# Clearing the dispatch rows from the row tile between the two first attentions

## The reference

```
mod = silu(c) @ ada_w + ada_b                 # six vectors of 1024: shift1, scale1, gate1, shift2, scale2, gate2
h = rmsnorm(x, norm1_g) * (1 + scale1) + shift1
qa, ka, va, fa, qb, kb, vb, ga, gb = split(h @ w_in)
o_fox = forgetting_attention(qa, ka, va, log_sigmoid(fa + b_forget))     # 8 heads of 64
o_sb  = stick_breaking_attention(qb, kb, vb)                             # 8 heads of 64
merged = sigmoid(ga) * (o_fox @ w_branch_fox) + sigmoid(gb) * (o_sb @ w_branch_sb)
x = x + gate1 * (merged @ w_out)
h2 = rmsnorm(x, norm2_g) * (1 + scale2) + shift2
y = hierarchical_moe(h2, ...)   # 16 experts, top 1 of 4 groups, top 2 of its 4 experts
x = x + gate2 * y
```

## Time and profile before

| what | value |
|---|---|
| time, median of 3 runs | 2736.78 us (2731.76 to 2738.37) |
| the profiled execution, its own time | 2731.88 us |
| its span, first to last instruction | 2730.3 us |
| PE busy | 2325.5 us, 85% |
| DVE, ACT, POOL busy | 1027.8, 831.5, 224.7 us |
| mean granted clock of PE | 0.918 |

### The profile page before, as it was taken

The page is one execution under the profiler, slowest core; times in us unless marked ns, Lnnn a source line. Parts: engine busy times, 40 slices in busy tenths (PEclk is TensorE's granted clock), DMA queues, the critical chain, the costliest instruction groups (busy, mean ns, idle before and its releaser), DMA issues.

```text
span 2730.3 us, 25692 instructions
## 1 busy us (share of the span) xinstructions
PE 2325.5 (85%) x9810; PEld 1662.0 (61%) x9810; DVE 1027.8 (38%) x1436; ACT 831.5 (30%) x1311; POOL 224.7 (8%) x255
## 2 busy tenths in 40 slices
PE   7898989829999956988859989959999976899996
PEld 4667666614444425855648778848865545777785
DVE  5635623431101014333542334442345554323444
ACT  3344511211111113213432223432245443222332
POOL 0420010010000011001010000030212100100000
PEclk9999899969999987979979999979999988899998
DMA  9213093227898971201012222222100002222221
GB/s 355 77 37 118 22 355 102 77 86 269 301 323 312 313 264 48 95 19 55 31 54 93 91 78 93 94 78 92 49 2 1 1 1 69 78 80 90 93 93 46
DMA packets 156312, 309.57 MB, mean 113 GB/s; under 512 B 17966, under 2 KB 19763, under 8 KB 156213
## 3 DMA queue, kind: packets, MB, share of 16 engines
q1 hardware_dynamic: 131308, 259.50, 27.9%
q0 software_dynamic: 11520, 41.95, 3.9%
q10 hardware_dynamic: 13388, 6.80, 1.0%
HBM read 277.02 MB, written 30.99 MB: 113 GB/s over the span
## 4 chain that ended last, share of the span: by engine, by line
PE 77%; DVE 10%; ACT 4%; issue 3%; DMA 2%; POOL 1%; ACTq 1%; POOLq 0%; DVEq 0%; SPq 0%; PEldq 0%
PE PB L1498 44%; PE PB L1855 8%; PE PB L1874 4%; PE PB L2137 3%; PE PB L1483 2%; PE PB L2113 1%; DVE WL L2230 1%; PE PB L1938 1%; PE PB L1915 1%; PE PB L1715 1%; PE PB L2114 1%; DVE CI L2853 1%; DVE NAT L2748 1%; DVE X L2750 1%; PE PB L2076 1%
## 5 line engine op out<-in xcount | busy, mean ns | idle before, releaser
L2230 DVE TENSOR_TENSOR WL<-RING,WH 128x1024 fp32r<-128x1024 f32 x232 | 288.4, 1243 | 736.7 <-ACT WH L826 460.3
L826 ACT CAST WH<-RING 128x1024 fp32r<-128x1024 f32 x232 | 243.6, 1050 | 932.2 <-PE PB L1498 864.1
L1498 PE MATMUL PB<-HTH,WH 128*128 128x512 f32 x1056 | 422.4, 400 | 60.7 <-DVE WL L2230 26.0
L1498 PE MATMUL PB<-HTL,WH 128*128 128x512 f32 x1056 | 418.5, 396 | 0.0
L1498 PE MATMUL PB<-HTH,WL 128*128 128x512 f32 x1056 | 418.0, 396 | 0.0
L1498 PE MATMUL PB<-WH,HTH 128*128 128x512 f32 (+1 forms) x832 | 323.9, 389 | 49.8 <-DVE HTL L2233 42.2
L1498 PE MATMUL PB<-WH,HTL 128*128 128x512 f32 (+1 forms) x832 | 322.0, 387 | 0.0
L1498 PE MATMUL PB<-WL,HTH 128*128 128x512 f32 (+1 forms) x832 | 321.6, 387 | 0.0
L1498 PEld LDWEIGHTS PB<-HTH,WH 128*128 128x128 f32 x1056 | 203.3, 192 | 108.0 <-issue 36.6
L1855 PE MATMUL PB<-RING,HT 128*128 128x512 f32 x512 | 226.1, 600 | 9.3 <-DVE HT L2622 7.6
L1498 PEld LDWEIGHTS PB<-HTH,WL 128*128 128x128 f32 x1056 | 202.8, 192 | 43.5
(11 more groups left out here) (453 smaller groups left out, 2846.7 us busy)
## 6 DMA issues: line engine op xcount, KB each, us to landing
RING<-in_mlp_w SPq DMA_DIRECT2D x64, 1024.0 KB, 5.3
RING<-in_expert_w_gate SPq DMA_DIRECT2D x32, 1024.0 KB, 5.6
RING<-in_expert_w_up SPq DMA_DIRECT2D x32, 1024.0 KB, 5.6
RING<-in_expert_w_down SPq DMA_DIRECT2D x32, 1024.0 KB, 6.7
BIG<-in_ada_w SPq DMA_DIRECT2D x10, 2048.0 KB, 11.8
RING<-in_w_in SPq DMA_DIRECT2D x20, 1024.0 KB, 5.6
dispatch_rows<-BIG POOLq DMA_DIRECT2D x24, 512.0 KB, 22.3
RING<-in_a_w_in SPq DMA_DIRECT2D x10, 1024.0 KB, 5.1
```

Of the source, the lines that this page charges most:

```text
L826: ins = nc.scalar.copy(WH[:, q % 2], halves_of(n, q))
L1498: yield pe.matmul(dst, lhs, rhs, start=(start and n == 0), stop=(stop_ and n == 2))
L2230: ins = V.tensor_tensor(WL[:, q % 2], halves_of(n, q), WH[:, q % 2].bitcast(F32), ALU.subtract)
```

## The change

The zero tile is now `ROW` in place of the last 1024 columns of `BIG`. POOL no longer waits for the end of the sb attention before it clears the zero tile and issues the 31 copies; it waits for the eight small transfers out of `ROW` (`fs_in`). Clearing `NAT[:, 0, :]` stays behind the sb attention and now stands behind the 31 copies on POOL. ACT waits for all 31 copies before it loads `gate1` into `ROW`.

```diff
@@ -347,7 +347,7 @@
-    ZERO = BIG[:, 15360:16384]
+    ZERO = ROW[:, :]
@@ -984,6 +984,9 @@
             act.wait_ge(mod_io, 32)
+            act.wait_ge(zero_out, 16 * (ROWS // P + 1 + SPARE - 2))
+            for m in range(2):
+                act.wait_ge(y_out[m], 16)
             gain_row(row_on_all(mod_dram[0, 2 * D:3 * D]))
@@ -1305,10 +1308,9 @@
             pool.wait_ge(fs_done, len(FOX_BLOCKS))
             nc.gpsimd.memset(SQ2[DH:P, :, :].bitcast(F32), 0.0).then_inc(f_pads, 1)
             pool.wait_ge(f_pads, 9)
-            pool.wait_ge(acc_done, GR["qkv"] + 8)
-            pool.wait_ge(sb_prod, len(SB_UNITS))
+            for par in range(2):
+                pool.wait_ge(fs_in[par], 16 * (NH1 // 2))
             nc.gpsimd.memset(ZERO, 0.0).then_inc(zeroed, 1)
-            nc.gpsimd.memset(NAT[:, 0, :], 0.0).then_inc(zeroed, 1)
             pool.wait_ge(zeroed, 2)
             for r in range(ROWS // P + 1):
                 pool.dma_start(disp[r * P:(r + 1) * P, :], ZERO).then_inc(zero_out, 16)
@@ -1317,6 +1319,9 @@
                 s = y_out[r % 2] if r < EXPERTS + 2 else zero_out
                 pool.dma_start(back[r * P:(r + 1) * P, :], ZERO).then_inc(s, 16)
+            pool.wait_ge(acc_done, GR["qkv"] + 8)
+            pool.wait_ge(sb_prod, len(SB_UNITS))
+            nc.gpsimd.memset(NAT[:, 0, :], 0.0).then_inc(zeroed, 1)
```

## The result

The changed kernel takes 2743.68 us (median of 13 runs, 2738.85 to 2747.30), the kernel before 2735.68 us (median of 13 timed with it, 2731.76 to 2743.83). The ratio is 1.0026, with a 95% interval of 1.0017 to 1.0034: slower by 7.1 us (4.6 to 9.3), and within the 0.3% that I took as the measure of "no change". The profiled execution took 2747.21 us, its span is 2745.6 us. It was one of the slowest of the changed kernel; what follows goes by stretches of the span, not by spans.

The account below looks back on a forecast made before the run. The prediction took PE to bound the kernel (busy 85% of the span). It summed -3.9 us at the gates and +11.2 at piece 9 to +7.3, on the median 2736.78 giving 2744 us, range 2733 to 2751.

Parts of the forecast that it names:

- Piece 9 beside the copies: Second projection: reads get 150 GB/s beside the copies, so piece 9 of `ada_w` lands at 252.5 instead of 236.9 us.
- Which other loads are covered: Around 204 to 260 us: piece 8 and chunks 9 and 10 may come late, but nothing waits for them.
- What is late then: From DVE's sums of piece 9 on: PE waits at part 20, and everything from part 22 stands 11.2 us later.
- The gates' gain: At the gates: one clearing less and piece 10 without copies beside it let PE restart earlier, -3.9 us.
- the low clock behind the gap: At the gates: PE's first 48 matmuls after the 3.7 us gap still lose 3.0 us to the low clock.
- a sign that it fails: At the gates: the prediction fails if PE's clock after the gap stays at 2.4 GHz.
- The sum: Whole kernel: -3.9 at the gates and +11.2 at piece 9 give +7.3 us.
- The copies' start: After the row sums leave `ROW`: first copy issued at about 199.5 us, bytes moving from about 204.5.
- What was to cost nothing: ACT's waits before the gain row and the late `NAT` clearing on POOL: both covered by the sb attention.
- Fairer turns: Rival at piece 9: equal bytes per queue, landing at 246.6, net +1.5 us, 2738; chance 0.17.
- Starvation: Rival at piece 9: it lands only once the copies are through, at 257, net +11.9 us, 2749; chance 0.17.
- No disturbance at all: Rival: copies disturb nothing at the new place, only the gates' gain stands, 2730 to 2733 us; chance 0.08.

Follow-up runs that it names:

- run 8: The changed kernel with piece 9 of `ada_w` read in 4 KB rows instead of 2 KB; piece 9 landed in 22.7 us; time not compared.
- run 4: The changed kernel with SP issuing piece 9 of `ada_w` ahead of chunk 11 of `w_in`; ratio 0.9985 against the kernel before, 2732.64 us.
- run 3: The changed kernel with POOL also waiting for piece 9 of `ada_w` to land before issuing the copies; ratio 0.9978 against the kernel before, 2731.03 us.
- run 7: The changed kernel with the first 12 copies left early and the other 19 behind piece 9's landing; ratio 0.9976 against the kernel before, 2730.09 us.
- run 5: The kernel before, zero tile still in `BIG`, with POOL waiting for piece 10 of `ada_w` to land before the copies; ratio 0.9990, 2732.99 us.

## Why the prediction was right

The sign and the mechanism were right, and so was the number (2744 against 2743.68); that it came so close is luck in part, as the sum below shows. Its steps, one by one:

- **Piece 9 beside the copies.** Predicted: lands 25.7 us after its issue. Measured: 26.4, 27.2 and 27.6. The step from the windows of 2 us to 150 GB/s held: beside the copies the reads had 0.30 MB in 2 us again.
- **Which other loads are covered.** Right: DVE went straight from its last step of the fox attention to piece 8 (215.27, 1.85 us later than before, of which 1.66 is the scatter ahead), and ACT waited for no chunk.
- **What is late then.** Predicted +11.2 us, with a gap of about 8.7 at part 20 and a small one before part 22. Measured: 9.26, 0.41 and 0.67, and +11.9 us; in the other two profiles of the change, 12.5 and 12.9 by the same landmark. PE's low clock behind the gap was hidden, as argued.
- **The gates' gain: right in kind, mis-sized.** Predicted -3.9; measured -6.4 in the first pair of profiles, and some -8 in the other two of the change. Two terms of it were off. The landing of an undisturbed piece 10 was taken from piece 8, 9.2 us; it was 7.7 to 8.0 in each run without copies beside it. Piece 8 was the wrong neighbour: it took 8.6 to 9.4 in all the profiles. And the low clock behind the gap was left at its full 3.0 us. PE took 12.8 us for the 48 matmuls in one profile of the change and 11.2 in the other two, in place of 13.9, so the clock cost 1.9 or 0.3 us. Windows over these 48 matmuls in the first and the second profile of the change (the last three figures are clock, DMA share and GB/s):

```profile
361.23:374.00 12.77, 12.77 (x49) 10.48 (x50) 5.37 (x6) 2.09 (x2) 0.00 (x0) 0.87 0.24 83
...
361.57:372.74 11.17, 11.17 (x49) 9.28 (x50) 5.37 (x6) 2.10 (x2) 0.00 (x0) 1.00 0.29 95
```

  In the second the clock stayed at 1.00 (2.4 GHz), which the prediction had named as a sign that it fails. It concerns this one term.
- **The sum.** +7.3 was predicted; the stretch gives +4.7 in the first pair of profiles (+3.9 on the means of three). Between them stand the two errors at the gates, 2.5 us together, less 0.7 at piece 9, and 0.8 us that the sb attention itself was shorter behind its new start (58.56 against 59.36 us from the fourth unit to the gates' first matmul), which I had not in the sum. The timed +7.1 is near the forecast only because it holds another 1 to 5 us, outside the stretch, that the prediction did not have. That part of the agreement is luck.
- **The copies' start.** The first copy was issued at 204.81, not 199.5: POOL stood for 4.62 us behind the clearing, where it had stood for 1.16 before. But the bytes then came 2.8 us after the issue, not 5, so they started at 207.6 in place of 204.5, and 1.66 us of these 3.1 are the scatter ahead. The copies ended at 261.2, not 256; piece 9 ran fully beside them all the same.
- **What was to cost nothing** did: ACT's gain row waited for nothing, the late clearing of `NAT` was done as soon as the sb attention ended.
- **The rivals.** Fairer turns: the windows speak against it, and piece 9 landed at 255 us, not 246.6. With reads in rows of 4 KB the bytes would have been nearly equal (run 8). Starvation: run 4 excludes it. No disturbance at all: that is what runs 3 and 7 made of it, by moving the copies, at 2731.0 and 2730.1 us, in its 2730 to 2733.

## What to carry to other kernels

A transfer of no urgency is not free because nothing waits for it: for as long as it drains, each load of another queue comes slower, here at 150 in place of 395 GB/s. So ask, when such work is moved, which load is issued while it drains and how much slack that load has; 3.6 us was not enough for a load that stood behind another in its queue, 3.15 MB in all. One wait in the issuing engine's program, on the landing of the last urgent load ahead of a stretch without loads, turned a loss of 7 us into a gain of 6. Where the background can't move, put the urgent load first in its queue (run 4). Rows as long as those of the background help less: they took 4 to 5 us off a landing that was 16 us late (run 8). And a difference of a few us in the time of the whole program need not lie in the stretch that was changed: here it lay in part where PE's clock went up and down.

## What was not expected of the hardware

- From POOL's first issue of a batch of copies to the first bytes on q0 it took 4.9 us in the kernel before, 2.8 in the change, 4.0 in run 3, 1.3 in run 5, and 2.7 and 1.1 for the two batches of run 7. Ahead of the issue, behind the clearing, POOL stood for 1.2 us in the kernel before and for 4.6 in the change. What sets these is open. In a row of issues each then takes 0.53 us.
- Two queues with work share the 16 engines by packets: with 2 KB reads and 4 KB writes 0.30 and 0.53 MB in 2 us, with 4 KB each 0.45 and 0.40. Copies of 128x512 by POOL, out of and into rows of 4 KB pitch, still showed data packets of 4096 bytes, as those of 128x1024 do.
- The same 2048 KB load by SP landed in 8.6 to 9.4 us at one place and in 7.7 to 8.0 at another, with no copies beside it, in every profile. SP's own instruction for it took 0.59 to 1.19 us at the first place and 0.37 to 0.38 at the second, which may be a part of the difference; the rest is open.
- After a gap of 2.30 us PE's clock fell in one execution of the changed kernel (48 matmuls in 12.8 us, mean clock 0.87), and after 2.44 and 2.31 us it stayed at 2.4 GHz in two others (11.2 us, 1.00).
